# The odd layer's gate projection on four column tiles of the TensorE array

## The reference, cut to what matters

```python
h = rms_norm(x, P['norm_mix'][l]) * (1 + sc1) + sh1           # 384 tokens x 1024
y = h @ P['w_in_odd'][oi]
z_s, xbc, dt, qkv, z_g, ga, gb = split_cols(y, ODD_SPLIT)     # dt: 16 columns, ga and gb: 8 each
...
xbc = centred_dwconv(xbc, P['ssd_conv_w'][oi], P['ssd_conv_b'][oi])   # 1024 channels
dts = jax.nn.softplus(dt + P['ssd_dt_bias'][oi])
...
qkv = centred_dwconv(qkv, P['gdn_conv_w'][oi], P['gdn_conv_b'][oi])   # 1536 channels
qg, kg = l2_norm(...) * GDN_DK ** -0.5, l2_norm(...)
beta = jax.nn.sigmoid(gb)
gdec = -jnp.exp(P['gdn_A_log'][oi]) * jax.nn.softplus(ga + P['gdn_dt_bias'][oi])
```

## Time and profile before

| what | value |
|---|---|
| time, median of 3 runs | 1316.23 us (1315.69 to 1316.28) |
| profiled execution, first to last instruction | 1311.2 us |
| PE busy | 1172.7 us, 89% |
| PEld busy | 679.5 us, 52% |
| DVE busy | 487.1 us, 37% |
| ACT busy | 350.9 us, 27% |
| mean granted TensorE clock | 0.960 of 2.4 GHz |

### The profile page before, as it was taken

How to read it: one execution, slowest core, us unless ns; L and a number is a source line. 1 busy time by engine, 2 the same in 40 slices (tenths; PEclk the granted TensorE clock), 3 DMA queues, 4 the chain that set the end, 5 groups by cost and what they waited for, 6 DMA issues and landing times. The chain is left out here.

```text
span 1311.2 us, 17725 instructions
## 1 busy us (share of the span) xinstructions
PE 1172.7 (89%) x6753; PEld 679.5 (52%) x6753; DVE 487.1 (37%) x1075; ACT 350.9 (27%) x750; POOL 115.6 (9%) x142
## 2 busy tenths in 40 slices
PE   5999987998999999788899999899889899988883
PEld 3555653345983333333556555788789533333333
DVE  3004473245152111001454885578732611110114
ACT  2101513246131111111234434443432211111111
POOL 1600000000001111101000000200000111111100
PEclk9899997999999999989998999999989899998997
DMA  9971387872859999998713120010165899999971
GB/s 363 316 301 47 121 327 292 327 268 86 340 209 347 416 415 416 409 416 357 243 65 128 64 97 0 2 34 2 67 252 196 337 375 417 410 418 397 399 296 65
DMA packets 87928, 329.15 MB, mean 251 GB/s; under 512 B 19183, under 2 KB 25497, under 8 KB 66976
## 3 DMA queue, kind: packets, MB, share of 16 engines
q1 hardware_dynamic: 72560, 297.40, 58.4%
q0 software_dynamic: 15280, 30.56, 6.7%
HBM read 320.04 MB, written 29.53 MB: 267 GB/s over the span
## 5 line engine op out<-in xcount | busy, mean ns | idle before, releaser
L1028 PE MATMUL psum<-wide,ring 128*128 128x384 f32 x704 | 240.6, 502 | 3.3 <-ACT wide L1786 1.9
L1028 PEld LDWEIGHTS psum<-wide,ring 128*128 128x128 f32 x704 | 167.3, 240 | 69.3 <-issue 6.9
L1416 PE MATMUL psum<-arena 128*64 128x512 f32 x568 | 158.2, 614 | 16.5 <-DMA arena<-in_moe_w_up 10.3
L1028 PE MATMUL psum<-ring,wide 128*128 128x512 f32 (+2 forms) x336 | 118.5, 511 | 0.0
L2543 DVE TENSOR_TENSOR arena<-arena,psum 128x256 f32<-128x256 f32 x34 | 14.3, 421 | 270.9 <-ACT arena L1943 270.9
L1416 PEld LDWEIGHTS psum<-arena 128*64 128x64 f32 x568 | 51.1, 141 | 117.7 <-issue 117.6
L1943 ACT ACTIVATE arena<-psum 128x256 f32<-128x256 f32 x34 | 13.1, 384 | 304.7 <-PE psum L1416 304.6
L1028 PEld LDWEIGHTS psum<-ring,wide 128*128 128x128 f32 x336 | 58.6, 194 | 53.5 <-issue 52.6
L1416 PE MATMUL psum<-ring,arena 128*64 128x512 f32 x320 | 73.8, 615 | 10.0 <-DMA ring<-in_moe_w_up 10.0
L1416 PE MATMUL psum<-wide,arena 128*64 128x512 f32 x160 | 72.2, 605 | 0.0
L2555 DVE TENSOR_SCALAR arena<-psum,share 128x512 f32<-128x512 f32 x34 | 25.5, 751 | 121.9 <-PE psum L1442 121.8
(11 more groups left out here) (552 smaller groups left out, 1648.2 us busy)
## 6 DMA issues: line engine op xcount, KB each, us to landing
ring<-in_ada_w SPq DMA_DIRECT2D x23, 2048.0 KB, 9.9
arena<-in_moe_w_gate SPq DMA_DIRECT2D x24, 1024.0 KB, 12.1
arena<-in_moe_w_up SPq DMA_DIRECT2D x24, 1024.0 KB, 20.4
arena<-in_moe_w_down SPq DMA_DIRECT2D x24, 1024.0 KB, 23.0
ring<-in_moe_w_gate SPq DMA_DIRECT2D x20, 1024.0 KB, 16.4
ring<-in_moe_w_up SPq DMA_DIRECT2D x20, 1024.0 KB, 19.7
ring<-in_moe_w_down SPq DMA_DIRECT2D x20, 1024.0 KB, 21.6
ring<-in_w_in_odd SPq DMA_DIRECT2D x7, 2048.0 KB, 8.2
```

Of the source, the lines that this page charges most:

```text
L1028: ins = mm(out, lhs(k), rhs(k), start=(k == 0), stop=(k == n - 1))
L1416: ins = mm(psum[half, 2 + s, :].rearrange("p (w f) -> p w f", w=2), hg[s][:, k, half], gate_up_of(UNITS[q][h], k), start=(k == 0), stop=(k ...
```

## The change

The 32 gate columns become the stationary operand and the 384 tokens move. The eight slices of the model width are dealt to four column tiles of the array, two to each: slices k and k + 4 add up in partitions 32 (k mod 4) and up of a new PSUM job, `dq`. ACT copies the 128 x 384 result to SBUF (`gate_quarters`, which is the buffer `rB`, free at that time). The four partial sums are added and turned into the old layout by three products, one for each token tile, in which 128 tokens of `gate_quarters` stand and a constant of 32 columns (`sum_quarters`, row mod 32 = column) moves; they fill `dg` as before. They come one step later, ahead of step 9, and with them ACT's and DVE's work on the gates. The constant makes `cst` 32 columns wider, 2627 for 2595.

```diff
@@ -132,6 +133,7 @@
+    c[:, C_SUM:C_SUM + 32] = row % 32 == np.arange(32)[None, :]
@@ -228,7 +230,8 @@
-    jobs += [("xb", i) for i in CONV_ORDER[:8]] + [("dg",)] + [("xb", i) for i in CONV_ORDER[8:12]] + [("cum", 1)]
+    jobs += [("xb", i) for i in CONV_ORDER[:8]] + [("dq",)] + [("xb", CONV_ORDER[8]), ("dg",)]
+    jobs += [("xb", i) for i in CONV_ORDER[9:12]] + [("cum", 1)]
@@ -280,7 +283,7 @@
-    last = [("zs", 2), ("xb", 3), ("xb", 7), ("xb", 11), ("xb", 15), ("xb", 19), ("zg", 2), ("dg",)]
+    last = [("zs", 2), ("xb", 3), ("xb", 7), ("xb", 11), ("xb", 15), ("xb", 19), ("zg", 2), ("dq",)]
@@ -1530,9 +1535,17 @@
             for n, i in enumerate(CONV_ORDER):
                 if n == 8:
                     w = wview(weight("odd", 7))
+                    b = issue("dq")
+                    for k in range(KD):
+                        quarter = slice(32 * (k % 4), 32 * (k % 4) + 32)
+                        ins = mm(b[quarter, 0:T], w[:, k, 0:32], hT[:, k, :], start=(k < 4), stop=(k >= 4),
+                                 tile_position=(0, quarter.start))
+                    ready(ins)
+                if n == 9:
                     b = issue("dg")
+                    pe.wait_ge(*taken("dq"))
                     for c in range(TILES):
-                        ins = contract(b[:, c * 32:c * 32 + 32], lambda k: hT[:, k, tok(c)], lambda k: w[:, k, 0:32], KD)
+                        ins = mm(b[:, c * 32:c * 32 + 32], gate_quarters[:, tok(c)], sum_quarters, start=True, stop=True)
                     ready(ins)
@@ -1975,6 +1988,9 @@
             for n, i in enumerate(CONV_ORDER):
                 if n == 8:
+                    act.wait_ge(*computed("dq"))
+                    take(fn(gate_quarters, bank("dq")[:, 0:T], ACT.Copy), "dq")
+                if n == 9:
                     act.wait_ge(*computed("dg"))
                     take(fn(dg.rearrange("p c n -> p (c n)"), bank("dg")[:, 0:TILES * 32], ACT.Copy), "dg")
@@ -2638,7 +2654,7 @@
             for n, i in enumerate(CONV_ORDER):
-                if n == 8:
+                if n == 9:
                     dve.wait_ge(*taken("dg"))
```

More of the change, by code:

```diff
@@ L103 @@
 C_ROW = C_TOKEN + TILES
-C_ALL = C_ROW + 2 * TILES
+C_SUM = C_ROW + 2 * TILES
+C_ALL = C_SUM + 32
 NOWHERE, NO_ROW = 512, 1024
@@ L359, in build @@
         y_at = cst[:, C_ROW:C_ROW + 2 * TILES].rearrange("p (w c) -> p w c", w=2)
+        sum_quarters = cst[:, C_SUM:C_SUM + 32]
         iota, token = cst[:, C_IOTA:C_IOTA + P], cst[:, C_TOKEN:C_TOKEN + TILES]
@@ L549, in build @@
         wA = carve(24)
+        gate_quarters = rB[:]
         base = used[0]
```

## The result

| | before | changed |
|---|---|---|
| median of the timed runs | 1316.02 us (13 runs, 1310.43 to 1323.72) | 1309.53 us (13 runs, 1303.96 to 1314.75) |
| profiled execution, span | 1311.2 us | 1308.5 us |
| mean granted clock in it | 0.960 | 0.957 |

The change makes the kernel faster by 0.4 to 0.5%, some 6 us.

A forecast was written before the change was run, and what follows sets the result against it. PE was taken as the bound: step 12 3.55 us earlier, less 1.7 for a clock fall, leaves 1.85; 1311.2 - 1.85 + 0.05 = 1309.4, plus 5.0 around it gives 1314.4 us. Range 1310.8 to 1317.0.

The forecast's parts named there:

- `dq`: On PE, eight products with 32 columns standing and 384 moving, in four column tiles: 1.5 us.
- the sums: On PE after step 8, three `dg` products, six records at full clock: 0.63 us.
- the clock at 1.00 through block and step 8: On PE, the fall at 701.52 should not happen, giving step 8 its 2.47 us back.
- the wait of the eighth `l2` product on the bank of `cum`: On PE, due at 725.3 but standing until 728.1, until DVE copies `cum` out: PE idles 2.8 us.
- step 12: On PE, begins at 728.85 against 732.40, 3.55 us earlier, with 3 of 6.5 us lost again.
- the fall behind the gap: On PE behind the idle gap, a stretch of 3.4 us at half clock, costing 1.7 us.
- With the 5.0 us around it.: Outside the profiled execution: 5.0 us added to its predicted 1309.4 us to give 1314.4 us.
- After 832 us everything follows PE: In the rest of the program, the gain is passed on; 1.2 us allowed for other falls of the clock.
- no overlap: Rival at `dq`: column tiles don't run side by side, `dq` takes 5.17 us; 1318.0 us, chance 0.10.
- no gap: Rival at the eighth `l2` product: bank of `cum` free in time, gain 6.5 us; 1309.8 us, chance 0.08.
- no fall: Rival behind the gap: the clock does not fall, all 3.55 us stay; 1312.7 us, chance 0.27.
- Not passed on: Rival: a stretch after 732 takes up the gain, or the clock falls in the block anyway; 1316.2 us, chance 0.10.

The follow-up runs named there:

- filler: Three products whose results nobody reads, added in the solve stage: kernel before with them 1311.06 us (ratio 0.9955), changed kernel with them 1309.97 us (0.9959).
- one_tile: Changed kernel with all eight slices in the first column tile and the sums over 32 partitions: 1314.23 us, ratio to before 1.0007.
- after_p4: The changed kernel without an edit, run for a further profile; its solve stage took the short way, and no timed median is given.
- cum_early: Changed kernel, but DVE copies `cum` out of its bank ahead of the taps of step 11: 1307.09 us, ratio to before 0.9939.
- interleaved: Kernel before, each of the eight wide products of step 8 followed by three of the 24 narrow ones: 1314.32 us, ratio 1.0011.
- step_earlier: Changed kernel with `dq` ahead of step 7, `dg` and all gate work ahead of step 8: 1307.39 us, ratio to before 0.9933.
- late_only: Kernel before with its 24 narrow products and the gate work moved ahead of step 9, nothing else changed: 1313.46 us, ratio 0.9998.
- before_again: The kernel before, measured once more without an edit: 1313.77 us, ratio to before 0.9991.
- same_step: Changed kernel with `dq`, `dg` and the gate work all ahead of step 8: 1309.35 us, ratio to before 0.9972.

## Why the prediction was wrong

The steps on the loop held, one by one. Measured from the block's start, predicted and found: `dq` 1.5 and 1.43; the sums 0.63 and 0.59; the clock at 1.00 through block and step 8, as found; the start of the `l2` products 23.4 and 23.5; ACT's copy of step 9 at 18.1 and 18.1; the wait of the eighth `l2` product on the bank of `cum`, 2.8 and 2.5 us; step 12 at 31.6 and 31.9; the fall behind the gap, there in all five profiles, 3.4 us long. The prediction had read three idle gaps for that fall, two of them with one; three more in the same trace, of 2.90, 2.40 and 1.80 us, had a fall behind the first two, so four of six. The sum for the span was 1309.4 and the profile has 1308.5.

Two terms of the sum failed, and both are about executions and not about instructions. The forecast of 1314.4 us was 4.9 us too high.

- **"With the 5.0 us around it."** The profiled execution was set equal to the median of the timed runs. What lies around a span is 2.0 us; the other 3 were the distance of this execution from a typical one. For the changed kernel the median lies 1.0 us above the profiled span (1309.53 and 1308.5), so this term alone is 4.0 of the 4.9 us; the other 0.9 are in the span. Which execution gets profiled is luck: this one had taken the short way through the solve stage, as half of them did. A sum made on it carries over to the median only if the median's extra stretches stay, and here they didn't.
- **"After 832 us everything follows PE"**, with 1.2 us for other falls of the clock. The term is mis-sized: the long way through the solve stage costs some 5.5 us (124.9 against 119.4 in the mean of three profiles each), is there in half the profiles of before, and in the mean the stage is 3.0 us shorter in the changed kernel. The rows that could have warned stand in every trace without filler: idle gaps, narrow products behind them. I looked at such gaps around the edit only.

Of the rivals, "no overlap" was excluded by the 1.43 us of `dq` against 5.28 in one_tile, "no gap" by the row of the gap, "no fall" by five profiles, though one_tile shows that such a gap can stay without a fall. "Not passed on" came out the other way: more than the loop's gain arrived.

What stays open is why the changed kernel is spared the long way, and with it some 4 of the 6 us of the median. Its fall behind the gap always comes at the same place of the program, 92.9 to 93.4 us ahead of `tk`, and 12.4 to 12.9 us into the solve stage, behind a wait of 1.71 us that every profile has, the clock falls again for 3.4 us in all five of its profiles (here after_p4, columns as in the earlier trace rows):

```profile
832.20:835.50 3.30, 3.05 (x38) 2.96 (x39) 1.51 (x3) 1.31 (x4) 1.13 (x2) 0.50 0.18 6
```

The three short profiles of before have this early fall too (14.2 to 14.4 us in), the three long ones don't. In before the place of the fall in the narrow products goes with it: it begins 122.2 to 122.3 us ahead of `tk` in the short ones and 122.6 to 122.8 in the long ones. An early fall makes PE itself late, so that the later wait could be short or split. That was seen, not tested, and it is not the whole rule: all five edited kernels with the long way had the early fall as well. Nor can it be the fall behind the gap that decides: one_tile has the gap without the fall and took the long way, cum_early has neither and took the short one. Zero of five against three of six is weak by itself, and the filler's 4.5 us in before and none in the changed kernel speak for the place, not for the reason, and with the uncertainty given above. That interleaved gained 2.1 us in the loop and nothing in the time (its profile has a solve stage of 126.4 us) fits, but is one profile.

## What to carry to other kernels

When work on one engine is made short, look at which bank or buffer the next same-numbered job shares with it, and who gives it back after how much queued work: here 3 of 6.5 us went into one bank that DVE read behind two sets of taps, and moving the copy up (cum_early) or the gate work one step earlier (step_earlier) brought them back on the loop. And where one kernel's executions spread by 1%, take several profiles of both before explaining a difference of a few microseconds: a stage with two lengths can weigh as much as the edit.

## What the runs showed of the hardware

- In the row of 24 products with 128 standing and 32 moving columns the profile has PE busy to 1.00 of the time, and yet the clock fell to 1.2 GHz in that row in all six profiles of before, and 0.6 us behind it in late_only; the same 24 spread among wide ones ran at 1.00, with no fall behind them in the loop (interleaved, one profile).
- The 48 records of these products took 5.27 us at 1.00 (late_only) and 6.18 us with the last 1.88 us at 0.50, so the fall cost 0.9 us there; step 8, with 4.94 us at 0.50, lost 2.5 us to it.
- The 32 Y1 records, behind waits at the same place, took 3.79 us at 2.4 GHz, or 6.3 to 7.1 us in stretches of 10.2 to 13.7 us at 1.2 GHz. How long the wait was did not tell which: 2.25 us at once without a fall (before_again), 1.36 us with one (same_step).
- Four column tiles of 32, each adding up two slices, gave a factor of 3.7 for 32-bit floats (5.28 to 1.43 us), entering and leaving the mode within it.
